# A decoder layer on one core: attention items taken in rounds of two, with the projection pieces between them placed by a new table

## What is computed

```python
def reference(x, ...):
    x = x + 0.5 * swiglu(rmsnorm(x, norm_ffn1), ffn1_w_in, ffn1_w_out)
    x = x + hybrid_mixer(rmsnorm(x, norm_mix), ...)
    x = x + 0.5 * swiglu(rmsnorm(x, norm_ffn2), ffn2_w_in, ffn2_w_out)
    return rmsnorm(x, norm_final)

def nsa_attention(q, q_rope, kc, vc, ks, vs, kw, vw, gates):   # 8 heads, 2 groups, head size 64
    ...   # per block of 128 queries
    p_c = masked_softmax(q @ kc)        # compressed keys, 31 of them
    p_s = masked_softmax(q_rope @ ks)   # selected blocks (all causal ones at this length)
    p_w = masked_softmax(q_rope @ kw)   # window
    return g0 * (p_c @ vc) + g1 * (p_s @ vs) + g2 * (p_w @ vw)

def dilated_group(q, k, v, dilation, span): ...   # 4 heads, 3 dilations, merged by their log-sum-exp
```

## Time and profile before

| | us |
|---|---|
| median of 3 runs | 1179.09 (1178.29 to 1181.44) |
| the profiled execution's own time | 1180.34 |
| its span, first to last instruction | 1178.5 |
| TensorE busy in it | 1165.9 (99%) |
| VectorE, ScalarE, GpSimd busy | 549.6, 395.4, 166.6 |

### The profile page before, as it was taken

One profiled execution on the slowest core, in us unless ns is written; L12 is line 12 of the kernel. 1 busy time (PEld: TensorE's weight loads), 2 busy tenths in 40 slices (PEclk: granted clock), 3 DMA queues, 4 the chain that ended last, 5 costly groups with the idle time before them and its releaser, 6 DMA issues.

```text
span 1178.5 us, 16661 instructions
## 1 busy us (share of the span) xinstructions
PE 1165.9 (99%) x6693; PEld 956.3 (81%) x6693; DVE 549.6 (47%) x824; ACT 395.4 (34%) x518; POOL 166.6 (14%) x196
## 2 busy tenths in 40 slices
PE   8999999999999999999999999999999999999997
PEld 6888888888888988777778888888888888888885
DVE  6444344463323467656655444553534444432222
ACT  6323323232223234443445422342332322322222
POOL 1000000000111481357660000021000000000000
PEclk9999999999999999999999999999999999999998
DMA  7332332323336831244231233332333233323321
GB/s 229 108 100 78 107 107 79 88 74 98 98 98 142 203 82 41 60 86 74 50 81 28 72 98 90 107 107 72 108 106 107 82 96 107 85 73 99 98 73 72
DMA packets 211299, 110.92 MB, mean 94 GB/s; under 512 B 32112, under 2 KB 207648, under 8 KB 211248
## 3 DMA queue, kind: packets, MB, share of 16 engines
q1 hardware_dynamic: 206832, 104.97, 33.3%
q0 software_dynamic: 4256, 5.09, 1.7%
q10 hardware_dynamic: 160, 0.14, 0.0%
HBM read 105.19 MB, written 2.10 MB: 91 GB/s over the span
## 4 chain that ended last, share of the span: by engine, by line
PE 97%; DVE 1%; DMA 0%; ACT 0%; issue 0%; SPq 0%; DVEq 0%; ACTq 0%
PE ps L1309 23%; PE ps L1310 22%; PE ps L1311 22%; PE ps L1426 7%; PE ps L1427 7%; PE ps L1428 7%; PE ps L1579 2%; PE ps L1502 2%; PE ps L1550 2%; PE ps L1521 1%; DMA x_nat<-in_x 0%; PE ps L1545 0%; PE ps L1595 0%; PE ps L1558 0%; PE ps L1489 0%; PE ps L1662 0%
## 5 line engine op out<-in xcount | busy, mean ns | idle before, releaser
L925 DVE TENSOR_TENSOR w_lo<-w_raw,w_hi 128x2048 fp32r<-128x2048 f32 (+5 forms) x116 | 225.8, 1947 | 392.9 <-ACT w_hi L687 392.7
L1309 PE MATMUL ps<-xg_hi,w_hi 128*128 128x512 f32 x992 | 389.6, 393 | 0.6 <-DVE xg_lo L1219 0.4
L1311 PE MATMUL ps<-xg_hi,w_lo 128*128 128x512 f32 x992 | 386.3, 389 | 0.0
L1310 PE MATMUL ps<-xg_lo,w_hi 128*128 128x512 f32 x992 | 386.2, 389 | 0.0
L687 ACT ACTIVATE w_hi<-w_raw 128x2048 fp32r<-128x2048 f32 (+3 forms) x104 | 180.5, 1735 | 337.5 <-PE ps L1311 214.9
L1309 PEld LDWEIGHTS ps<-xg_hi,w_hi 128*128 128x128 f32 x992 | 186.2, 188 | 41.9 <-issue 3.7
L1311 PEld LDWEIGHTS ps<-xg_hi,w_lo 128*128 128x128 f32 x992 | 186.2, 188 | 39.2
L1310 PEld LDWEIGHTS ps<-xg_lo,w_hi 128*128 128x128 f32 x992 | 186.3, 188 | 37.5
L1426 PE MATMUL ps<-p_hi,w_hi 128*128 128x512 f32 x352 | 137.0, 389 | 0.0
L1428 PE MATMUL ps<-p_hi,w_lo 128*128 128x512 f32 x352 | 136.9, 389 | 0.0
L1427 PE MATMUL ps<-p_lo,w_hi 128*128 128x512 f32 x352 | 136.9, 389 | 0.0
(11 more groups left out here) (194 smaller groups left out, 1134.4 us busy)
## 6 DMA issues: line engine op xcount, KB each, us to landing
w_raw<-in_ffn_w_in SPq DMA_DIRECT2D x86, 512.0 KB, 5.0
w_raw<-in_w_in SPq DMA_DIRECT2D x32, 512.0 KB, 5.3
w_raw<-in_ffn_w_out SPq DMA_DIRECT2D x32, 384.0 KB, 3.6
w_raw<-in_ffn_w_out SPq DMA_DIRECT2D x32, 320.0 KB, 4.1
w_raw<-in_w_in SPq DMA_DIRECT2D x24, 256.0 KB, 4.4
w_raw<-in_w_out SPq DMA_DIRECT2D x8, 512.0 KB, 4.1
x_nat<-in_x SPq DMA_DIRECT2D x8, 256.0 KB, 5.0
w_raw<-in_w_branch_nsa SPq DMA_DIRECT2D x8, 256.0 KB, 4.0
```

What stands on the lines that cost most here:

```text
L925: lo = V.tensor_tensor(w_lo[:, s, c], w_raw[:, s, c], w_hi[:, s, c].bitcast(F32), ALU.subtract)
L1309: mm(out, ah, bh, start=(first and i == 0), stop=False)
L1310: mm(out, ah, bl, start=False, stop=False)
L1311: last = mm(out, al, bh, start=False, stop=(final and i == len(pairs) - 1))
```

## The change

The items are taken in pairs, called rounds here: n is even, and a round handles n and n+1. Per round TensorE does transpositions(n), piece(n), transpositions(n+1), scores(n+2), scores(n+3), values(n), values(n+1), piece(n+1). ScalarE does copy(n), [high part of a weight unit], copy(n+1), exp(n+2), exp(n+3), then the copies of bank 6, then splits of y. VectorE reads chunk(n-1), splits both low halves of a weight unit, reads chunk(n), then prepares n+2 and n+3 and then scales n+2 and n+3. The table of pieces is new: two pieces per step up to item 9 (there a chunk has two pieces), then one and three (of four) in turn, or whole chunks in the rounds of `WHOLE`. The cmp item moves from index 4 to index 5. The compressed values of head 0 are added with one matmul per group in place of two.

```diff
--- before.py
+++ after.py
@@ -340,7 +340,7 @@
         ITEMS = []
         for hh in range(HPG):
             ITEMS += [("nsa", hh, i, qts) for qts in ((0, 1), (2,), (3,)) for i in range(2)]
-        ITEMS.insert(4, ("cmp", 0))
+        ITEMS.insert(5, ("cmp", 0))
         N_NSA = len(ITEMS)
         LAST_OF = [ITEMS.index(("nsa", hh, 1, (TT - 1,))) for hh in range(HPG)]
         for hp in range(2):
@@ -443,14 +443,10 @@
 
         PIECES = [piece for c in range(N_PRE, len(CH)) for piece in pieces_of(c)]
         N_QKV = sum(c < N_CH3 for c, _, _ in PIECES)
-        QKV_STEPS, LAST_STEP = N_NSA, len(ITEMS) - 1
+        WHOLE = (10, 12, 16, 20, 22)
         FILL, done = {}, 0
-        for n in range(-1, len(ITEMS)):
-            if done == len(PIECES):
-                break
-            goal = (N_QKV * (n + 1) / QKV_STEPS if n < QKV_STEPS else
-                    N_QKV + (len(PIECES) - N_QKV) * (n + 1 - QKV_STEPS) / (LAST_STEP - QKV_STEPS))
-            count = 2 if n == -1 else min(4, max(1, round(goal - done)))
+        for n in range(-1, len(ITEMS) - 1):
+            count = 2 if n < 10 else 4 if n - n % 2 in WHOLE else (1, 3)[n % 2]
             took = [piece for piece in PIECES[done:done + count] if piece[0] == PIECES[done][0]]
             FILL[n] = (took[0][0], (took[0][1], took[-1][2]))
             done += len(took)
@@ -472,9 +468,8 @@
         for n in FILL:
             if filled(n) is not None and ends_unit(filled(n)):
                 unit = CH[filled(n)][1] + 2
-                wanted = min([m for m in FILL if CH[FILL[m][0]][1] == unit], default=n + 3)
                 for half in range(2):
-                    SPLITS.setdefault(n + 1 + half + (wanted > n + 3), []).append((unit, half))
+                    SPLITS.setdefault(n + 2 - n % 2 + half, []).append((unit, half))
 
         def by_class(name):
 
@@ -821,17 +816,26 @@
             nc.scalar.activation(y_parts[c][0][:, :], y[:, c, :], ACT.Copy).then_inc(y_hi_ready, 1)
 
         def act_attend(act, a, b):
-            for n in range(a, b):
-                act_copy_probs(act, n)
-                if n + 2 < b:
-                    act_exp(act, n + 2)
-                if n > a and ends_pair(n - 1) is not None:
-                    act_y(act, n - 1)
-                c = filled(n - 1)
+            def split_after(n):
+                c = filled(n)
                 if c is not None and ends_unit(c):
                     act_split(act, MIX0 + CH[c][1] + 2)
-                if splits_y(n) is not None:
-                    act_split_y(act, splits_y(n))
+
+            for n in range(a, b, 2):
+                act_copy_probs(act, n)
+                split_after(n - 1)
+                if n + 1 < b:
+                    act_copy_probs(act, n + 1)
+                for nn in (n + 2, n + 3):
+                    if nn < b:
+                        act_exp(act, nn)
+                for nn in (n, n + 1):
+                    if nn < b - 1 and ends_pair(nn) is not None:
+                        act_y(act, nn)
+                split_after(n)
+                for nn in (n, n + 1):
+                    if splits_y(nn) is not None:
+                        act_split_y(act, splits_y(nn))
             act_y(act, b - 1)
             act_split_y(act, 5)
 
@@ -1189,21 +1193,21 @@
         def dve_attend(dve, a, b):
             dve.wait_ge(gate_ready, 1)
             dve_factor(dve, a)
-            for n in range(a, b):
-                c = filled(n - 1)
-                if c is not None:
-                    dve_chunk(dve, c)
-                if n + 1 < b:
-                    dve_factor(dve, n + 1)
-                if n + 2 < b:
-                    dve_prepare(dve, n + 2)
-
-                for unit, half in SPLITS.get(n, ()):
-                    dve_split(dve, MIX0 + unit, half=half)
-                if splits_y(n - 1) is not None:
-                    dve_split_y(dve, splits_y(n - 1))
-            for unit, half in SPLITS.get(b, ()):
-                dve_split(dve, MIX0 + unit, half=half)
+            dve_factor(dve, a + 1)
+            for n in range(a, b, 2):
+                if filled(n - 1) is not None:
+                    dve_chunk(dve, filled(n - 1))
+                for nn in (n, n + 1):
+                    for unit, half in SPLITS.get(nn, ()):
+                        dve_split(dve, MIX0 + unit, half=half)
+                    if splits_y(nn - 2) is not None:
+                        dve_split_y(dve, splits_y(nn - 2))
+                if filled(n) is not None:
+                    dve_chunk(dve, filled(n))
+                for step in (dve_prepare, dve_factor):
+                    for nn in (n + 2, n + 3):
+                        if nn < b:
+                            step(dve, nn)
 
         @block.vector
         def _(dve):
@@ -1553,10 +1557,9 @@
 
         def pe_cmp_values(hh, opens):
             rows = slice(hh * NC, hh * NC + NC)
-            for at, w in ((0, T),) if opens else ((0, 3 * P), (3 * P, P)):
-                for g in range(2):
-                    last = mm(ps[g * DH:g * DH + DH, 6, at:at + w], v_cmp[rows, g, :],
-                              cmp_probs_t[rows, g * T + at:g * T + at + w], start=opens, stop=False)
+            for g in range(2):
+                last = mm(ps[g * DH:g * DH + DH, 6, :], v_cmp[rows, g, :], cmp_probs_t[rows, g * T:g * T + T],
+                          start=opens, stop=False)
             return last
 
         def pe_values(pe, n):
@@ -1604,17 +1607,20 @@
 
         def pe_attend(pe, a, b):
             pe_fill(pe, -1)
-            for n in range(a, b):
+            for n in range(a, b, 2):
                 pe_transpose_probs(pe, n)
-                if n + 2 < b:
-                    pe_scores(pe, n + 2)
-                late = n > a + 1 and ITEMS[n - 1][0] == "cmp"
-                if n > a and not late:
-                    pe_values(pe, n - 1)
                 if n in FILL:
                     pe_fill(pe, n)
-                if late:
-                    pe_values(pe, n - 1)
+                if n + 1 < b:
+                    pe_transpose_probs(pe, n + 1)
+                for nn in (n + 2, n + 3):
+                    if nn < b:
+                        pe_scores(pe, nn)
+                for nn in (n, n + 1):
+                    if nn < b - 1:
+                        pe_values(pe, nn)
+                if n + 1 in FILL:
+                    pe_fill(pe, n + 1)
 
             pe.wait_ge(lo_ready, MIX0 + U_GM[2] + 1)
             pe.wait_ge(proj_read, len(CH))
```

## The result

The changed kernel takes 1217.99 us (median of four runs, 1216.6 to 1218.84) against 1180.26 us of the kernel before beside it (1178.29 to 1181.47): 1.0316 times as long, with a 95% interval of 1.0302 to 1.0331. It is slower, as forecast, but by 37.7 us where 22.8 were worked out; 1202 was predicted, and 1218 lies above the range of 1191 to 1211. Its profiled execution took 1217.53 us, with a span of 1215.7 us against 1178.5 before.

The account below looks back on a forecast made before the run. TensorE, busy 99% of the span, was taken as the bound. Bank copies 21.5 + smaller waits 3.7 + clock 5.6 - passages 8.0 = 22.8 us on 1180.3 gave 1203.1, as a median 1202; range 1191 to 1211.

Parts of the forecast that it names:

- Bound and sign: Whole kernel: TensorE busy 99% of the span, so only shorter steps could gain; slower, at a chance of 0.94.
- The passages: TensorE, attention stage: three fewer tile-shape changes per round, 0.17 us each, save 8.0 us over 16 rounds.
- The bank copies: Rounds of items 6, 12, 18, 24, 28: second values wait for ScalarE's bank 6 copy behind two exps, 21.5 us.
- The smaller waits: Attention stage: TensorE waits for the first chunk, bank 7 reads, the cmp item and one split round, 3.7 us together.
- The clock: TensorE behind the bank-copy waits: four of five bring the granted clock down, 1.4 us each, 5.6 us.
- the 8.5 us worked out beside it: Clock cost by the skill's rule: all five long idle times bring a fall, 1.7 us each.
- The rival of two slow times per stall: Attention stage: up to 6 us more clock cost; with VectorE's halves stretched 3 to 5 us, 1207 to 1213; chance 0.13.
- Above 8 us it is slower: Deciding sum of all waits and slow clocks: under 4.5 us faster by over 0.3%, above 8 us slower.

Follow-up runs that it names:

- the shifted rounds: Changed kernel with rounds shifted by one item (item 0 alone, then (1, 2), (3, 4)) and the first chunk read early: 1180.85 us.
- the alternating kernel: The fastest kernel with scores and values of a round's two items alternating instead of both scores, then both values: 1183.91 us.
- the fastest: The shifted kernel with pieces offset so that a chunk ends with the small piece ahead of the second transpositions: 1178.53 us.

## Why the prediction was wrong in size

- **Bound and sign: right.** TensorE had no idle time to give, so the change could only save passages and add waits. It was slower, as the chance of 0.94 said.
- **The passages: right, and nearly so in size.** 8.0 us were taken; the steps give some 7.2, since scores or values in a row save 0.13 to 0.15 us and not 0.17. A round of two dilated items took 11.91 us (654.55 to 666.46) with 0.25 us of waiting in it, against 12.20 us (637.93 to 650.13) for two such items before. The Trainium skill (TensorEngine Tiling (Array Packing), Key Properties) says that a change of the tiling mode drains the engine, but gives no price. The traces agree: 0.13 to 0.17 us where the tile shape changes and about nothing between transpositions and pieces, which are both 128*128.
- **The bank copies: right.** 21.5 us predicted, 22.0 measured, at the five predicted places, and the chain in the round of item 18 within 0.5 us at each end. The copy moved ahead of the exps, the piece put between and the shifted rounds each took the waits away.
- **The smaller waits: mis-sized too.** 3.7 predicted, 8.7 measured. The read of bank 7 costs 0.25 to 0.47 us in nearly every round, where "0.25 us in four rounds and 0.05 in some eight" was taken. The step at fault is "the read is over 0.2 + 0.69 us after the last matmul, six transpositions take 0.7 and eight 0.9": between pieces they take 0.57 and 0.79 us, and the next matmul starts 1.04 us after the last one, 0.15 us after the read's end. The first chunk cost 1.8 in place of 1.3 us, and the reads behind the compressed item and in one other round 0.97 and 1.28 in place of 0.5 each.
- **The clock: the step that failed.** "I take it that four of the five bring the clock down, and that part of each slow time falls into the idle time: 4 x 1.4 = 5.6 us." Measured were 13.9 us. All five waits brought it down, and the small one at the first chunk too. In three of the five the slow time did not begin within the idle time but just behind its end, so that TensorE worked through all of it, and in four of the five it lasted 6.8 us, twice the one fall of the earlier trace rows from which the price was taken. The rule that the prediction cites from the Trainium skill (TensorE: Matmul & The Clock Gate, Part 1), that only activity holds the throttled state off, was closer on which waits count (five, not four); the 8.5 us worked out beside it had the same short slow time in them. The rival of two slow times per stall, held at 0.13 together with a longer chain, is the one that came, in four of five.
- **The sum again, with what was measured.** 22.0 + 8.7 + 13.9 - 7.2 = 37.4 us, in place of 21.5 + 3.7 + 5.6 - 8.0 = 22.8. Of the 16 us between 1202 and 1218, the clock is 8.3, the smaller waits 5.0, the passages 0.8, the copies 0.5, and 1.2 us are the kernel before itself, whose median was 1179.1 us when the prediction was made and 1180.3 beside the changed kernel.
- **A slip without effect.** "Above 8 us it is slower" doesn't fit the 0.3% that the rivals start from: by that measure the change is slower above 11.5 us of waits and slow clocks. The 44.6 us measured lie far beyond either.

What stays open: why some falls last 3.4 us, others 6.8, and one 10.2, and what decides whether a wait of 1.3 to 1.6 us brings one. The runs show that the same wait can go with different falls (at item 6: 6.8 us behind it in the changed kernel, 10.2 from within it with the first chunk read early); no run here was made to set it.

## What to carry to other kernels

When two accumulations into one bank come to stand back to back, the copy between them is on the path with everything that its engine does first: put the copy ahead of that engine's other work, or put a piece of independent work between, which here won back some 30 of the 37.7 us either way. Price an idle time of three microseconds or more on TensorE at itself plus 1.5 to 3.2 us, as the five waits here cost, and look for the granted clock in the stretch behind it as well as in it. Steps of one tile shape in a row were worth 0.13 to 0.17 us per passage saved, and that is easily eaten by one read that lost its cover: count who reads the bank that the next step needs before counting passages.

## What was not expected of the hardware

- The granted clock stayed at 1.00 through an idle stretch of over 4 us (492 to 497 us, 0.86 us of work in 5) and fell to 0.50 as work began, for 6.8 us. It does so three times in the changed kernel; filling the waits with useless matmuls removes the falls and gives back 11.65 us. It is no rule: in the kernel with the first chunk read early the fall in the same round began 2.3 us ahead of the wait's end.
- A wait of 1.8 us (444.4 to 446.2 us) was enough for a fall of 3.4 us, while the earlier trace rows have a stretch of 2 us with 0.44 us of work that kept 1.00, and two waits of 1.44 and 0.58 us in the alternating kernel brought none.
- Four scalings of 128x128 on VectorE at the first item took 3.12 us in the shifted kernel and 3.06 in the one with only the compressed item moved (its first transpositions waited 1.49 us in place of 0.3), 2.04 us in the kernel before and in the fastest, and 1.01 us in the alternating one, whose VectorE and GpSimd programs are those of the fastest. In all of them GpSimd rotates a chunk at that time. Where the scalings took 1.01 us, GpSimd's next instruction (L627) began only at 442.44, 0.2 us ahead of their end. In the fastest kernel it began at 441.68, and they took 2.04; in the shifted one two instructions lay beside them, from 441.52 and 442.96, and they took 3.12. So the time went with what GpSimd did beside them, about 1 us for each instruction; no run was made to show that as the cause.
